# Tile-by-tile starts behind the norms of a two-block network on one core

## What is computed

```python
for l in range(2):
    x = x + 0.5 * swiglu_ffn(rms_norm(x, ffn1_norm[l]), ffn1_w_in[l], ffn1_w_out[l])
    h = rms_norm(x, mix_norm[l])
    uv, c_q, c_kv, k_rope, z, xbc, dt_raw, gates = split(h @ w_in[l])
    y_a = gmlp_mixer(uv, ...)            # gelu, norm, causal spatial product
    y_b = mla_mixer(c_q, c_kv, k_rope, ...)   # latents normed, 8 heads, causal attention
    y_c = ssd_mixer(z, xbc, dt_raw, ...)      # short convolution, chunked scan
    g = sigmoid(gates)
    merged = g[0] * (y_a @ w_branch[l, 0]) + g[1] * (y_b @ w_branch[l, 1]) + g[2] * (y_c @ w_branch[l, 2])
    x = x + merged @ w_out[l]
    x = x + 0.5 * swiglu_ffn(rms_norm(x, ffn2_norm[l]), ffn2_w_in[l], ffn2_w_out[l])
```

## Time and profile before

| | us |
|---|---|
| median of 3 runs (lowest, highest) | 1966.35 (1964.43, 1967.27) |
| the profiled execution | 1966.4 |
| its span | 1964.6 |
| TensorE matmul busy (97%) | 1913.6 |
| of it `keep_busy`, L306 (43.8 + 18.4) | 62.2 |
| TensorE not busy (span less busy) | 51.0 |
| VectorE busy (47%) | 932.7 |
| ScalarE busy (36%) | 709.2 |
| POOL busy (4%) | 77.9 |

### The profile page before, as it was taken

How to read it: one execution, slowest core, us unless ns; L and a number is a source line. 1 busy time by engine, 2 the same in 40 slices (tenths; PEclk the granted TensorE clock), 3 DMA queues, 4 the chain that set the end, 5 groups by cost and what they waited for, 6 DMA issues and landing times.

```text
span 1964.6 us, 25874 instructions
## 1 busy us (share of the span) xinstructions
PE 1913.6 (97%) x10898; PEld 1571.9 (80%) x10898; DVE 932.7 (47%) x1166; ACT 709.2 (36%) x813; POOL 77.9 (4%) x145
## 2 busy tenths in 40 slices
PE   9999999999999999999999999999999999999998
PEld 8998585577999899985855678998787975759996
DVE  4545134467554445441335674545667431134453
ACT  5543213143554345432131343554223111124542
POOL 0000000000000000000000002000371100000000
PEclk9999999999999999999899999999998899999999
DMA  6545434343553565454344337636444213326353
GB/s 236 175 139 192 147 124 153 129 137 120 193 172 127 192 215 171 142 193 143 128 145 133 132 108 138 229 117 211 149 135 115 65 65 128 129 86 215 128 182 128
DMA packets 192246, 293.06 MB, mean 149 GB/s; under 512 B 7218, under 2 KB 126804, under 8 KB 192164
## 3 DMA queue, kind: packets, MB, share of 16 engines
q1 hardware_dynamic: 189908, 287.72, 43.3%
q0 software_dynamic: 1936, 4.14, 2.0%
q10 hardware_dynamic: 320, 0.01, 0.0%
HBM read 289.49 MB, written 2.36 MB: 149 GB/s over the span
## 4 chain that ended last, share of the span: by engine, by line
PE 89%; DVE 6%; DMA 2%; ACT 2%; issue 1%; POOL 0%; DVEq 0%; SPq 0%; ACTq 0%; POOLq 0%
PE acc L221 17%; PE acc L223 17%; PE acc L222 17%; PE acc L189 15%; PE acc L253 7%; PE acc L416 2%; PE acc L2389 1%; PE acc L203 1%; PE acc L2697 1%; DMA ring<-in_ffn_w_out 1%; DMA ring<-in_ffn_w_in 1%; DVE w_lo L387 1%; PE acc L2094 1%; PE acc L1168 1%; PE turn L314 1%
## 5 line engine op out<-in xcount | busy, mean ns | idle before, releaser
L387 DVE TENSOR_TENSOR w_lo<-ring,w_hi 128x2048 fp32r<-128x2048 f32 x160 | 362.8, 2290 | 271.4 <-ACT w_hi L383 271.0
L221 PE MATMUL acc<-xT_hi,w_hi 128*128 128x256 f32 x1680 | 477.4, 284 | 6.9 <-DVE w_lo L387 6.9
L222 PE MATMUL acc<-xT_lo,w_hi 128*128 128x256 f32 x1680 | 476.3, 284 | 0.0
L223 PE MATMUL acc<-xT_hi,w_lo 128*128 128x256 f32 x1680 | 476.2, 283 | 0.0
L383 ACT ACTIVATE w_hi<-ring 128x2048 fp32r<-128x2048 f32 x160 | 302.1, 1913 | 217.2 <-DMA ring<-in_ffn_w_out 110.2
L221 PEld LDWEIGHTS acc<-xT_hi,w_hi 128*128 128x128 f32 x1680 | 323.5, 193 | 7.3 <-issue 7.1
L222 PEld LDWEIGHTS acc<-xT_lo,w_hi 128*128 128x128 f32 x1680 | 323.5, 193 | 0.1
L223 PEld LDWEIGHTS acc<-xT_hi,w_lo 128*128 128x128 f32 x1680 | 323.5, 193 | 0.0
L189 PE MATMUL acc<-ring,xT 128*128 128x512 f32 (+2 forms) x736 | 300.4, 567 | 0.8 <-DVE xT L2677 0.8
L189 PEld LDWEIGHTS acc<-ring,xT 128*128 128x128 f32 x736 | 139.1, 190 | 152.3 <-issue 139.7
L221 PE MATMUL acc<-w_hi,hT_hi 128*128 128x512 f32 x440 | 172.9, 393 | 4.4 <-DVE w_lo L387 4.4
(11 more groups left out here) (507 smaller groups left out, 2065.8 us busy)
## 6 DMA issues: line engine op xcount, KB each, us to landing
ring<-in_ffn_w_in SPq DMA_DIRECT2D x88, 1024.0 KB, 5.6
ring<-in_w_in SPq DMA_DIRECT2D x48, 1024.0 KB, 5.0
ring<-in_ffn_w_out SPq DMA_DIRECT2D x44, 1024.0 KB, 4.9
ring<-in_w_branch SPq DMA_DIRECT2D x12, 1024.0 KB, 5.0
ring<-in_w_out SPq DMA_DIRECT2D x12, 1024.0 KB, 5.0
ring<-in_w_gate SPq DMA_DIRECT2D x11, 1024.0 KB, 5.2
ring<-in_w_up SPq DMA_DIRECT2D x11, 1024.0 KB, 6.6
ring<-in_w_down SPq DMA_DIRECT2D x11, 1024.0 KB, 5.0
```

The source lines that it names most:

```text
L221: pe.matmul(o, a_hi, wh, start=start, stop=False)
L222: pe.matmul(o, a_hi, wl, start=False, stop=False)
L223: return pe.matmul(o, a_lo, wh, start=False, stop=stop)
L387: vec.tensor_tensor(w_part(w_lo, r), raw_part(c0, r), w_part(w_hi, r).bitcast(F32), ALU.subtract).then_inc(f.lo, 1)
```

## The change

- **Norms.** All transposes of a norm but those of the mixer's come behind the product before. The next product's first half-block (two feature tiles of 128) goes over token tile 0 first, in matmuls of 128 columns: four wait for the first quarter of `xT`, four for the second; then the transposes of tile 1, then the rest. This is `first_gate` for FFNs and `turned_half_pe` for the second block's first product and the cross attention's query. VectorE (`add_norm_vec`) adds tile 1 ahead of the copies of tile 0 where `late=True`. Around it `first_split_act` and `first_split_vec` (the first weight split of the FFN) stand between the tiles' steps (`between`). `keep_busy` goes from all of these places but the program's start, where 18 stay, and from the mixer; one is added in the cross attention (5 to 6).
- **Loads.** The down projection's chunks wait only for the split of the chunk that was in the slot, no more for its products. The first four chunks of the stage behind an FFN likewise wait for splits (`raw_freed`). `part_hi` becomes four deep and `part_lo` gives way to `ring_lo`, the rest written over the chunk itself, so the tail's splits no longer wait for products.
- **The mixer's middle.** The query latent is normed by itself, ahead of the key/value latent; `dt_pe` is cut in two, each inside the second convolution group; `gm_turn_pe` moves behind that group, and with it VectorE's `gm_vec3`.
- **The mixer's tail.** The softmax steps go one branch earlier on every engine, branch 1 comes half by half around them, and the last branch, the gated sum and the output projection go tile by tile.

```diff
+        def load(sync, c, src, k, n, freed=None):
+
+            sync.wait_ge(*(freed or (products_done, c + 1)))
             sync.dma_start(slot(c, k, n), src).then_inc(landed[c % RING], 16)
...
-            if e >= 2:
-                wait_products(act, c - 2)
-            act.activation(hi[:, e % 2], slot(c, k, n), ACT.Copy).then_inc(s.hi, 1)
...
+            act.activation(hi[:, e % RING], slot(c, k, n), ACT.Copy).then_inc(s.hi, 1)
...
-            vec.tensor_tensor(lo[:, e % 2], slot(c, k, n), hi[:, e % 2].bitcast(F32), ALU.subtract).then_inc(s.lo, 1)
+            vec.tensor_tensor(slot_lo(c, k, n), slot(c, k, n), hi[:, e % RING].bitcast(F32), ALU.subtract).then_inc(s.lo, 1)
...
+        def turned_half_pe(pe, G, c, norm):
+
+            norm_pe(pe, norm, tiles=(0,))
+            for i in range(2):
+                wait_chunk(pe, c + i)
+            wait_acc_free(pe, G, 0)
+            for m in range(MT):
+                for f in range(2):
+                    if m == 0 and f == 1:
+                        norm_pe(pe, norm, tiles=(1,))
+                    for k in range(KD):
+                        if f == 0 and k % 4 == 0:
+                            pe.wait_ge(norm.vec, norm.turned(2 * m + k // 4))
+                        pe.matmul(acc[bank(G, 0)][:, f * TOK + m * P:f * TOK + (m + 1) * P],
+                                  slot(c + k // 4, 4, 512)[:, k % 4, f * P:(f + 1) * P], xT[:, k, m * P:(m + 1) * P],
+                                  start=(k == 0), stop=(k == KD - 1))
...
+                if between and f % 2:
+                    between(pe, f // 2)
...
+            add(vec, 0)
+            tile(0)
+            if late:
+                add(vec, 1)
+            turned(0)
+            turned(1)
+            if not late:
+                add(vec, 1)
+            tile(1)
+            if between:
+                between(vec)
+            turned(2)
+            turned(3)
...
+            return f.lo, RING + N_IN + KF // 2 - RING + j + 1
...
-                sync.wait_ge(products_done, c0 + r + 1)
+                if after and r < RING and type(i) is int:
+                    sync.wait_ge(*raw_freed(after, r))
+                elif r < N_IN:
+                    sync.wait_ge(products_done, c0 + r + 1)
                 sync.wait_ge(f.lo, r + 1 + RING * i)
                 sync.dma_start(raw_part(c0, r), src).then_inc(landed[(c0 + r) % RING], 16)
...
-                keep_busy(pe, acc[bank(G0, 0)], 4)
-                pe.wait_ge(n.vec, n.v0 + 8)
-                wait_chunk(pe, c0)
-                for ft in range(2):
-                    for k in range(KD):
...
+                for m in range(MT):
+                    for ft in range(2):
+                        if m == 0 and ft == 1:
+                            norm_pe(pe, n, tiles=(1,))
+                        for k in range(KD):
+                            if ft == 0 and k % 4 == 0:
+                                pe.wait_ge(n.vec, n.turned(2 * m + k // 4))
+                            ins = pe.matmul(acc[bank(G0, 0)][:, ft * TOK + m * P:ft * TOK + (m + 1) * P],
+                                            raw_part(c0, 0)[:, k, ft * P:(ft + 1) * P], xT[:, k, m * P:(m + 1) * P],
+                                            start=(k == 0), stop=(k == KD - 1))
...
+            def dt_pe(pe, m):
+
+                pe.wait_ge(cq.vec, 6)
...
-                pe.wait_ge(qs.vec, 50)
-                keep_busy(pe, turn[2], 2)
                 pe.wait_ge(qs.vec, 52)
...
+            def last_branch_pe(pe):
+
+                b = BRANCHES[2]
+                pe.wait_ge(tail.vec, 4)
+                for m in range(MT):
+                    for n in range(2):
+                        ins = split_chunk_pe(pe, tail, G_BR + 4 + n, m, C_BR + 4 + n, 6 + n, yT_hi[:, b], yT_lo[:, b], part_hi)
+                        ins.then_inc(tail.pe if m == 0 else products_done, 1)
+                        if m == 1 and n == 0:
+                            merged_pe(pe, 0)
...
+                b = BRANCHES[2]
+                vec.wait_ge(br.vec, 2 * n + m + 1)
+                wait_acc_read(vec, G_GATE + 2 * b + n, m)
+                if m == 0:
+                    vec.wait_ge(tail.pe, n + 1)
+                else:
+                    wait_products(vec, C_BR + 4 + n)
+                G = G_BR + 4 + n
...
-                keep_busy(pe, turn[2], 5)
                 turned_group_pe(pe, G_XBC0, C_XBC0, xT, 4, 512)
                 cq_pe(pe)
+                turned_group_pe(pe, G_XBC1, C_XBC1, xT, 4, 520, between=dt_pe)
                 gm_turn_pe(pe)
-                dt_pe(pe)
-                turned_group_pe(pe, G_XBC1, C_XBC1, xT, 4, 520)
...
-                split_group_pe(pe, tail, G_GATE + 5, C_SPLIT, 0, normed_hi, xT_rest, part_hi, part_lo, 2)
-                branch_pe(pe, 0)
-                branch_pe(pe, 1)
...
+                branch_pe(pe, 0, 0)
+                branch_pe(pe, 0, 1)
                 qs_pt_pe(pe)
+                branch_pe(pe, 1, 0)
                 qs_pv_pe(pe)
-                branch_pe(pe, 2)
-                merged_pe(pe)
...
+                last_branch_pe(pe)
                 for n in range(2):
-                    split_group_pe(pe, tail, G_WO + n, C_WO + 2 * n, 8 + 2 * n, xT_hi, xT_rest, part_hi, part_lo, 2,
-                                   for_x=(n == 1))
+                    for m in range(MT):
+                        pe.wait_ge(tail.vec, 6 + 2 * m)
+                        for i in range(2):
+                            if n == 0 and m == 0 and i == 1:
+                                merged_pe(pe, 1)
+                            ins = split_chunk_pe(pe, tail, G_WO + n, m, C_WO + 2 * n + i, 8 + 2 * n + i, xT_hi[:, 4 * i:4 * i + 4],
+                                                 xT_rest[:, 4 * i:4 * i + 4], part_hi, i == 0, i == 1)
+                            if m == 1:
+                                ins.then_inc(products_done, 1)
+                        if n == 1 and m == 0:
+                            ins.then_inc(tile0_done, 1)
...
                 branch_in_act(act, 0)
+                tail_part_act(act, 2, 3)
+                qs_act3(act, 0)
+                qs_act3(act, 1)
+                gate_act(act, 5)
                 branch_in_act(act, 1)
...
+                tail_part_vec(vec, 2, 3)
+                qs_vec5(vec, 0)
                 branch_in_vec(vec, 1)
-                tail_part_vec(vec, 3, 4)
-                branch_gate_vec(vec, 0)
...
-                add_to_x(vec, C_WO + 3, G_WO, 1.0, 3 * l + 2)
-                norm_vec(vec, n2, col[:, R["ffn2"]:R["ffn2"] + 8])
-                first_split_vec(vec, f2, C_FFN2)
+                add_norm_vec(vec, lambda e, m: add_tile_to_x(e, m, C_WO + 3, G_WO, 1.0, 3 * l + 2), n2, col[:, R["ffn2"]:R["ffn2"] + 8],
+                             late=True, between=lambda e: first_split_vec(e, f2, C_FFN2))
...
-                norm_pe(pe, n1, tiles=(1,) if l > 0 else (0, 1), busy=7 if l > 0 else 18)
...
+                if l == 0:
+                    keep_busy(pe, turn[0], 18)
...
-                norm_pe(pe, n2, busy=5)
-                ffn_pe(pe, f2, n2, C_FFN2, G_FFN2, lambda e: norm_pe(e, n_next, tiles=(0,)), asides={4: params2_pe, 6: s5_c_pe} if l == DEPTH - 1 else {})
+                ffn_pe(pe, f2, n2, C_FFN2, G_FFN2, lambda e: None, asides={4: params2_pe, 6: s5_c_pe} if l == DEPTH - 1 else {})
...
-            norm_pe(pe, nm, tiles=(1,), busy=7)
-            pe.wait_ge(nm.vec, nm.v0 + NORM_DONE)
-            turned_group_pe(pe, G_K2, C_K2, xT, 4, 512)
+            turned_half_pe(pe, G_K2, C_K2, nm)
+            turned_group_pe(pe, G_K2, C_K2, xT, 4, 512, f0=2)
...
-            group_pe(pe, G_XO + 1, C_XO + 2, xT, (4, 4), 512, for_x=True)
-            norm_pe(pe, n3, busy=5)
+            tile_pe(pe, G_XO + 1, C_XO + 2, xT, 0, tile0_done)
+            tile_pe(pe, G_XO + 1, C_XO + 2, xT, 1)
```

334 lines of the change are left out of this document (167 added, 167 removed).

## The result

| | us |
|---|---|
| before, median of 4 runs (lowest, highest) | 1965.39 (1962.49, 1967.27) |
| after, median of 4 runs (lowest, highest) | 1915.10 (1910.84, 1916.95) |
| ratio, 95% interval | 0.9742 (0.9721 to 0.9763) |
| profiled execution after, its span | 1915.92, 1914.2 |
| TensorE busy, of it filler | 1863.4, 14.4 |

The changed kernel was measured beside the kernel before in two later series again: 0.9768 (0.9752 to 0.9784; 1916.0 against 1960.2) and 0.9763 (0.9744 to 0.9783; 1916.4 against 1961.4). So the change is worth 44 to 50 us; 43 were forecast. One of the five executions of the changed kernel in the first of these two, the profiled one, took 2341.5 us at a mean granted clock of 0.748; the comparison leaves it out, and the profile that repeats the changed kernel is that of the last series.

What follows compares the result with a forecast made beforehand. TensorE holds 89% of the chain of waits, so only its idle and filler can be won. The terms sum to -43.1 us, from the profiled 1966.4 us to 1923 us, range 1910 to 1938.

Steps and rivals of the forecast that it cites:

- Norm boundaries: Less idle and filler at norms: three FFNs -9.3 us, between layers -3.9, second block -3.5, cross attention -2.7.
- The walk: Step-by-step timing of the engines' queues; at the boundary into the second block, idle 1.2 us instead of 4.9.
- Rival A: The clock falls at each of six norm boundaries for 3.4 us, 10 us in all: 1933 us; chance 17%.
- E: TensorE still waits for both tiles' chains at each boundary; only loads, latent norm and dt gain: 1948 us; chance 3%.
- Latent norm and dt: Mixer's middle: fillers, idle and the L904 wait go, -7.4 us; clock no longer falls at the dt matmuls, -6.7.
- The -6.7: Mixer's middle, both layers: cutting dt in two ends the clock's fall, 1.7 + 3.0 + 2.0 us.
- Loads: Down projection: five waits for a split weight go because loads wait only for the slot's split, -4.5 us.
- The tail: Mixer's tail: filler and idle of 10.6 us a layer give way to new waits, -9.4 us; clock +4.0.
- New idle 5.9 a layer: Mixer's tail: TensorE waits 1.6 and 3.3 us among softmax transposes, 0.8 at the last branch, 0.2 at the output projection.
- The clock: Mixer's tail: half speed for 3.4 us behind the softmax transposes, +2.0 us in each layer.
- The second table load: ScalarE in the tail: new load of 1.3 us ahead of the last gate's sigmoids, taken without a drain.
- The wait beside POOL's DMAs: FFN whose loads collide with POOL's parameter DMAs: its 6.9 us stall stays, may shrink by 2 or grow by 3.

Runs made afterwards that it cites:

- run 1: The kernel before with every filler taken out that the change takes out, and nothing else; 1979.9 us, ratio 1.009 to the kernel before.
- run 6: The changed kernel with VectorE's scaling of tile 1 ahead of branch 1's input split and six copies moved ahead, in both tails; 1905.0 us, ratio 0.9715.
- Run 3: The changed kernel with the 32 eight-column dt matmuls in one piece ahead of the second convolution group; 1925.6 us, ratio 0.9819 to the kernel before.
- run 2: The kernel before with only the down projection's chunk loads waiting for the slot's split, not its products; 1955.8 us, ratio 0.9977.

## Why the prediction was right

**Norm boundaries: right.** The walk gave 0.95 idle ahead of the first product, then 0.2 ahead of the second transposes; it was 1.20 and none. The sum, 1.2, and the terms (-9.1, -3.7, -3.7, -3.1) agree within 0.4. Rival A (the clock falls here) did not come; E (both chains waited for) neither. The reading that 2.0 us of transposes and idle do not lower the clock, taken from the earlier trace rows, held at all six. The Trainium skill, "TensorE: Matmul & The Clock Gate", Part 4, says of transposes that they do not count as busy in the same way. The boundaries don't refute it: without filler and with 2.43 us of idle ahead of the transposes the clock did fall (run 1). Nor does run 6 decide it, though it speaks against the rule for so short a run: behind its 2.8 us of transposes without idle the clock stayed at 1.00.

**Latent norm and dt: right in mechanism, one size by luck.** -7.9 and -7.0 for -7.4 and -6.7. Run 3 shows that the thin run was the cause, but gives 2.36 a layer, 4.7 in all. The -6.7 took layer 1's 5.64 and 17.05 from one profile, and run 2's profile, with the same code there, had 3.64 and 15.75. So 3.3 of the term came from that one profile; the table above meets it again because its side of before is that same profile.

**Loads: right in mechanism, small in size.** -5.9 by stage times for -4.5, and 5.8 in run 2. Each FFN got shorter by its wait and 0.2 to 0.3 more. In the timeline a matmul starts 0.16 to 0.25 us ahead of the modelled end of the one before when nothing is waited for, and a wait's row counts from that end, so the lost overlap isn't in it. The term should have been 4.5 plus five overlaps; it was read from the waits alone. That the overlap is the whole difference is argued, not tried.

**The tail: right in mechanism, the sizes off.** "New idle 5.9 a layer" was 4.8: 1.39 and 3.00 for 1.6 and 3.3, and 0.41 for 0.8 at the last branch, with no wait ahead of the output projection. That is 2.2 of the 3.0 us by which the term missed. The clock cost what was taken, 2.2 and 1.7 us for 2.0 each; some 0.7 stays open. The walk through ScalarE's and VectorE's queues named the first wait's cause, and run 6 showed it. The second table load, in ScalarE's timeline after:

```profile
423.95 1.28 ACT L1370 ACT_TABLE_LOAD   x1
425.24 1.09 ACT L1370 ACTIVATE big<-acc 128x512 f32<-128x512 f32 x2
```

The sigmoid follows 0.01 behind it. Here too there is no drain of the size that the Trainium skill gives, "ScalarE: Activation LUTs", What ACT_TABLE_LOAD costs.

**What the sum lacked.** The second block (-3.3) had no term. Part of it is half speed that comes and goes without an edit. But in the last series' profile, with as much half speed there as before the change, the block was still 1.8 us shorter than before; what that is stays open. The wait beside POOL's DMAs grew by 1.6 and its stage by 1.1, inside the bounds given (2 less to 3 more). The reason given, loads that collide with POOL's DMAs, holds: the late chunk set the end of the wait, though the profile names "issue".

**How near the total is.** The forecast of 1923 stands on the profile of 1966.4 us, and the kernel before took 1960.2 to 1961.4 in the later series, the changed kernel 1915 to 1916 in all three. The gain of 44 to 45 there is nearer to the 43 than the 50 of the first. Part of this nearness is luck: by runs 2 and 3 the dt term was too large by some 2 us, and by the table the loads and the tail, together, too small by 4.4.
